# Modulation sums moved from TensorE to VectorE in a two-block transformer kernel, and gathered in the feed-forward stages and one MLP

## What is computed

```python
s_lat, s_ctx = silu(c), silu(c_ctx)[None, :]
for i in range(2):
    sh1, sc1, g1, sh2, sc2, g2 = split(s_lat @ ada_w[i] + ada_b[i], 6)       # ada_w[i]: 1024 x 6144
    csh1, csc1, cg1, csh2, csc2, cg2 = split(s_ctx @ ada_w[i] + ada_b[i], 6)
    a_l = rms_norm(h_lat, norm_g[i, 0]) * (1 + sc1) + sh1
    ...
```

## Time and profile before

| | |
|---|---|
| time, median of 3 runs | 1859.87 us (1859.79 to 1861.17) |
| the profiled execution | 1859.17 us, of which its span is 1857.4 us |
| mean granted clock of TensorE, as a share of full | 0.984 |
| busy: TensorE, weight loads, VectorE, ScalarE, GpSimd | 1758.9, 1600.3, 810.8, 890.4, 1169.6 us |
| read from memory | 295.89 MB, 160 GB/s over the span |
| groups L951 (ada, 768 records) and L959 (turn, 48 records) | 53.1 and 6.1 us busy |

### The profile page before, as it was taken

How to read it: one execution, slowest core, us unless ns; L and a number is a source line. 1 busy time by engine, 2 the same in 40 slices (tenths; PEclk the granted TensorE clock), 3 DMA queues, 4 the chain that set the end, 5 groups by cost and what they waited for, 6 DMA issues and landing times.

```text
span 1857.4 us, 32633 instructions
## 1 busy us (share of the span) xinstructions
PE 1758.9 (95%) x12970; PEld 1600.3 (86%) x12970; DVE 810.8 (44%) x1929; ACT 890.4 (48%) x1462; POOL 1169.6 (63%) x768
## 2 busy tenths in 40 slices
PE   7899999999999999999999979999999989989997
PEld 6888899999998888999999867777777777689997
DVE  6677445313366784353233662121212275642223
ACT  6535547445666345464445863131313353554443
POOL 6876678788888775778788515444434434158884
PEclk9999999999999999999999989999999999999999
DMA  6643365655556434656655514333334433135552
GB/s 235 196 134 126 125 228 199 224 207 182 182 194 195 134 115 139 241 182 216 227 182 182 166 57 148 133 136 131 137 130 148 183 114 131 40 101 191 185 183 80
DMA packets 83416, 299.06 MB, mean 161 GB/s; under 512 B 9152, under 2 KB 11456, under 8 KB 83008
## 3 DMA queue, kind: packets, MB, share of 16 engines
q1 hardware_dynamic: 81648, 294.02, 46.4%
q10 hardware_dynamic: 1616, 2.95, 0.5%
HBM read 295.89 MB, written 1.05 MB: 160 GB/s over the span
## 4 chain that ended last, share of the span: by engine, by line
PE 78%; DVE 9%; POOL 5%; ACT 3%; issue 3%; DVEq 2%; DMA 0%; ACTq 0%; SPq 0%
PE bank L937 23%; PE bank L940 22%; PE bank L941 22%; POOL wlo L886 5%; PE bank L951 2%; PE bank L1117 1%; ACT whi L1356 1%; PE bank L1133 1%; PE bank L1180 1%; DVE split_acts L1814 1%; PE bank L1103 1%; DVE acts L2026 1%; DVE acts L2067 1%; PE bank L1183 1%; PE bank L1184 1%
## 5 line engine op out<-in xcount | busy, mean ns | idle before, releaser
L886 POOL TENSOR_TENSOR wlo<-raw,whi 128x256 fp32r<-128x256 f32 (+1 forms) x756 | 1163.8, 1564 | 666.8 <-ACT whi L1356 666.5
L937 PE MATMUL bank<-split_acts,whi 128*128 128x256 f32 (+1 forms) x3492 | 1059.9, 304 | 30.0 <-DVE split_acts L1814 16.6
L940 PE MATMUL bank<-split_acts,whi 128*128 128x256 f32 (+1 forms) x3492 | 1047.4, 300 | 0.0
L941 PE MATMUL bank<-split_acts,wlo 128*128 128x256 f32 (+1 forms) x3492 | 1047.1, 300 | 0.0
L937 PEld LDWEIGHTS bank<-split_acts,whi 128*128 128x128 f32 x3492 | 670.5, 192 | 81.3 <-issue 28.9
L1356 ACT ACTIVATE whi<-raw 128x1024 fp32r<-128x1024 f32 x459 | 482.4, 1055 | 509.9 <-PE bank L937 331.1
L941 PEld LDWEIGHTS bank<-split_acts,wlo 128*128 128x128 f32 x3492 | 671.1, 192 | 20.8
L940 PEld LDWEIGHTS bank<-split_acts,whi 128*128 128x128 f32 x3492 | 671.3, 192 | 20.2
L2449 DVE SCALAR_TENSOR_TENSOR acts<-bank,acts 128x256 f32<-128x256 f32 x104 | 47.4, 482 | 227.5 <-PE bank L941 227.5
L2463 DVE TENSOR_SCALAR acts<-bank 128x512 f32<-128x512 f32 (+1 forms) x64 | 35.6, 558 | 204.7 <-PE bank L941 197.6
L1814 DVE TENSOR_TENSOR split_acts<-bank,split_acts 128x256 fp32r<-128x256 f32 (+1 forms) x212 | 97.9, 462 | 49.4 <-ACT split_acts L1500 20.7
(11 more groups left out here) (275 smaller groups left out, 1595.6 us busy)
## 6 DMA issues: line engine op xcount, KB each, us to landing
raw<-in_stream SPq DMA_DIRECT2D x555, 512.0 KB, 3.8
acts<-in_x SPq DMA_DIRECT2D x1, 1024.0 KB, 6.3
acts<-in_ctx ACTq DMA_DIRECT2D x1, 1024.0 KB, 7.4
acts<-in_const ACTq DMA_DIRECT2D x1, 1024.0 KB, 5.0
out<-acts SPq DMA_DIRECT2D x8, 128.0 KB, 2.0
acts<-in_const SPq DMA_DIRECT2D x1, 711.0 KB, 8.3
acts<-in_p ACTq DMA_DIRECT2D x2, 256.0 KB, 4.0
acts<-in_const ACTq DMA_DIRECT2D x1, 320.0 KB, 2.9
```

The lines of the kernel that those rows point to most:

```text
L886: last = nc.gpsimd.tensor_tensor(wlo[slot][:, cols], raw[source][:, cols], whi[slot][:, cols].bitcast(F32), ALU.subtract)
L937: first = nc.tensor.matmul(out_ap, w_hi, hi_act(k), start=(k == 0), stop=False)
L940: nc.tensor.matmul(out_ap, w_hi, lo_act(k), start=False, stop=False)
L941: last = nc.tensor.matmul(out_ap, w_lo, hi_act(k), start=False, stop=(k == k_tiles - 1))
```

## The change

TensorE's ada and turn tiles go. A modulation chunk ("mod") now holds two k steps of half a part, two times 128 x 512, so that four chunks (SUM_CHUNKS) make one of 24 halves. VectorE reads it from its raw slot and adds silu times weight into a running sum per side (0 context, 1 latents; halves from 16 on have side 1 alone). In block 1 the running sums are in PSUM banks 6 and 7, and the last step writes to SBUF; in block 2 they are in SBUF, in v2. The slot is freed by VectorE (mod_used). When a half is done, a "sum" tile two tiles later adds the 128 partitions on TensorE: one matmul per 128 columns and side, the sums as weights, a column of ones as moving operand. VectorE adds the bias.

The chunks are no longer in heads, middle stages and attention. Each layer of block 1 has 24 in its feed-forward stages, before hg 0,1 to 0,9, dn 0,1 to 0,6 and hg 1,0 to 1,8; block 2's first MLP has 48, before nearly every w1 and w2 tile. The bytes fetched are the same. c_square has two banks in place of four, `opening_gains` comes later in layer 1, and eight columns of constants that only the turn used are gone.

```diff
@@ -79,26 +79,23 @@
     + [("kn", j) for j in range(4)] + [("qn", j) for j in range(4)] + [("qr", 0), ("qr", 1)]
     + [("rotq", 0), ("rotq", 1)])
-ADA_TILES = DEPTH * 6 * D // 256
-LAYER_ADA = 12
-PLACES = 4
-
-
-def with_modulation(tiles, places, first, flush=()):
-
-    out, n, turned = [], first, first // PLACES
-    for t in tiles:
+SUM_CHUNKS = 4
+SUM_BEHIND = 2
+
+
+def with_sums(tiles, places):
+
+    out, n, due = [], 0, []
+    for i, t in enumerate(tiles):
+        if due and due[0][1] <= i:
+            out.append(("sum", due.pop(0)[0]))
         for _ in range(places.get(t, 0)):
-            if n // PLACES > turned:
-                out.append(("turn", turned))
-                turned += 1
-            out.append(("ada", n))
+            out.append(("mod", n))
             n += 1
-        if t in flush and n // PLACES > turned:
-            out.append(("turn", turned))
-            turned += 1
+            if n % SUM_CHUNKS == 0:
+                due.append((n // SUM_CHUNKS - 1, i + SUM_BEHIND))
         out.append(t)
-    assert turned * PLACES == n
+    assert not due
     return out, n
...
@@ -114,16 +111,14 @@
 FIRST_PRODUCT = {"mix": ("u", 0), "ffn": ("hg", 0, 0), "ple": ("pg", 0)}
 for _name in ("ffn", "ple"):
     TAIL_TILES.insert(TAIL_TILES.index(FIRST_PRODUCT[_name]) + 1, ("ss", _name))
-HEAD_TILES, _n = with_modulation(HEAD_TILES, {("u", 1): 1, ("gl", 0): 1, ("ss", "q"): 1, ("rotk", 0): 1},
-                                 0, flush=(("kn", 2),))
-MID_TILES, _n = with_modulation(MID_TILES, {("g", 2, 0): 1, ("g", 2, 2): 1, ("g", 2, 4): 1, ("g", 2, 6): 1}, _n,
-                                flush=(("y", 2, 7),))
-TAIL_TILES, _n = with_modulation(TAIL_TILES, {("hg", 0, 3): 1, ("hg", 0, 6): 1, ("hg", 0, 9): 1, ("dn", 0, 3): 1}, _n,
-                                 flush=(("dn", 0, 6),))
-assert _n == LAYER_ADA
+FFN_PLACES = {**{("hg", 0, j): 1 for j in range(1, 10)}, **{("dn", 0, n): 1 for n in range(1, 7)},
+              **{("hg", 1, j): 1 for j in range(9)}}
+ALL_TAIL_TILES, LAYER_MODS = with_sums(TAIL_TILES, FFN_PLACES)
+TAIL_TILES = [t for t in ALL_TAIL_TILES if t[0] != "mod"]
 FF_TILES = TAIL_TILES[TAIL_TILES.index(("hg", 0, 0)):TAIL_TILES.index(("dn", 1, 0))]
 PLE_TILES = TAIL_TILES[TAIL_TILES.index(("pg", 0)):]
-TILES = HEAD_TILES + MLA_FILL + FOX_FILL + MID_TILES + TAIL_TILES
+ALL_LAYER_TILES = HEAD_TILES + MLA_FILL + FOX_FILL + MID_TILES + ALL_TAIL_TILES
+TILES = [t for t in ALL_LAYER_TILES if t[0] != "mod"]
...
@@ -185,19 +176,20 @@
 def chunk_reach(tiles, spans, order, at):
-    reach, needed, adas, read = {}, 0, 0, 0
+    reach, needed, mods, read = {}, 0, 0, 0
     for t in tiles:
-        end = -(-spans.get(t, (0, 0))[1] // CHUNK_ATOMS)
+        first, to = spans.get(t, (0, 0))
+        end = -(-to // CHUNK_ATOMS)
         read = max(read, end)
-        if t[1][:2] != ("py", 0):
+        if t[1][:2] != ("py", 0) and to > first:
             needed = max(needed, end)
-        adas += ADA_CHUNKS * (t[1][0] == "ada")
+        mods += t[1][0] == "mod"
         last = at[t] if needed == read else order.index(("split", needed - 1))
         r = min(last + AHEAD, len(order) - 1)
         while r + 1 < len(order):
             kind, n = order[r + 1]
             freed_by, m = order[r + 1 - RING] if r + 1 >= RING else ("split", 0)
-            if kind == "split" and (n >= needed + SLOTS_AHEAD or (freed_by == "ada" and m >= adas)):
+            if kind == "split" and (n >= needed + SLOTS_AHEAD or (freed_by == "mod" and m >= mods)):
                 break
             r += 1
         reach[t] = r
@@ -251,15 +243,15 @@
     + [("ss", 1, 0)] + Q_TILES + K_TILES + V_TILES
     + [("o", n) for n in range(KT)]
     + [("ss", 1, 1)] + mlp_tiles(1) + [("ss", "last")])
-TILES2, _n = with_modulation(
-    TILES2,
-    {("w1", 0, 0, 0): 2, ("w1", 0, 0, 4): 1,
-     **{(w, 0, q, j): 1 for q in range(QUARTERS) for w in ("w1", "w2") for j in (0, 4) if (w, q) != ("w1", 0)},
-     ("w2", 0, 3, 2): 1, ("w2", 0, 3, 6): 1, ("w1", 0, 3, 2): 1,
-     ("q", 4): 1, ("q", 6): 1, ("k", 0): 1, ("k", 1): 1},
-    DEPTH * LAYER_ADA, flush=(("ss", 1, 0), ("k", 2)))
-assert _n == ADA_TILES
-BEFORE2 = modulation_before(TILES2)
+
+
+MLP_PLACES = [((w, 0, q, j), 1) for q in range(QUARTERS)
+              for w, js in (("w1", range(2, 7) if q == 0 else range(1, 6)),
+                            ("w2", range(8 if q < 2 else 7 if q == 2 else 5))) for j in js]
+ALL_TILES2, _n = with_sums(TILES2, dict(MLP_PLACES))
+assert DEPTH * LAYER_MODS + _n == DEPTH * 6 * KT
+BEFORE2 = modulation_before(ALL_TILES2)
+TILES2 = [t for t in ALL_TILES2 if t[0] != "mod"]
...
@@ -419,10 +410,11 @@
 def modulation_atoms(a, m):
-    group, k = divmod(m, PLACES * ADA_CHUNKS)
-    layer, part = divmod(group, 6)
-    w = a["ada_w_2"][layer][k * P:(k + 1) * P, part * D:(part + 1) * D]
-    return [w[:, i * P:(i + 1) * P] for i in range(KT)]
+    half, pair = divmod(m, SUM_CHUNKS)
+    layer, part = divmod(half // 2, 6)
+    at = part * D + half % 2 * 512
+    return [a["ada_w_2"][layer][k * P:(k + 1) * P, at + i * P:at + (i + 1) * P]
+            for k in (2 * pair, 2 * pair + 1) for i in range(4)]
...
@@ -587,6 +579,14 @@
     return ("mla", n) if n < STEPS // 2 else ("fox", n - STEPS // 2)
+LAYER_SUMS = LAYER_MODS // SUM_CHUNKS
+
+
+def sum_of(half):
+
+    return half // 2, half % 2, (0, 1) if half < 16 else (1,)
+
+
...
@@ -709,7 +708,7 @@
         low[0] = H_AT
         h = take(4096)
         pr2, pt2 = take(1024), take(1024)
-        rows2 = v2[:, 0:256]
+        mod_sums = [[v2[:, (2 * i + s) * 512:(2 * i + s + 1) * 512] for s in range(2)] for i in range(2)]
         pooled_sq = [sq2[:, i * 256:(i + 1) * 256] for i in range(KT)]
...
         k_rstd, logits2 = x, squares
-        c_square = [bank[4], bank[5], bank[6], bank[7]]
+        c_square = [bank[4], bank[5]]
+        mod_parts = [bank[6], bank[7]]
         x_squares = [bank[5], bank[6]]
...
@@ -862,7 +862,7 @@
                 if kind == "split":
                     sp.wait_ge(lo_ready, n + 1)
                 else:
-                    sp.wait_ge(ada_used, n + 1)
+                    sp.wait_ge(mod_used, n + 1)
             for c in range(N_CHUNKS - RING):
...
-            def modulation(b):
-
-                for part in range(ADA_CHUNKS):
-                    c, k = RAW_OF[("ada", Cursor.ada)], Cursor.ada % KT
-                    Cursor.ada += 1
-                    pe.wait_ge(raw_in[c % RING], (c // RING + 1) * 16)
-                    for strip in range(4):
-                        last = nc.tensor.matmul(b[32 * strip:32 * strip + 32, 0:256], silu_c[:, 2 * k:2 * k + 32],
-                                                raw[c % RING][:, strip * 256:(strip + 1) * 256],
-                                                start=(part == 0), stop=(part == ADA_CHUNKS - 1))
-                    last.then_inc(ada_used, 1)
-                return last
-
-            def turn_rows(b, rows):
-                for i in range(2):
-                    last = nc.tensor.matmul(b[:, 8 * i:8 * i + 8], rows[:, i * P:(i + 1) * P], C("strips"),
-                                            start=True, stop=True)
+            def sum_parts(b, half):
+
+                pe.wait_ge(mod_summed, half + 1)
+                for s in sum_of(half)[2]:
+                    for i in range(4):
+                        last = nc.tensor.matmul(b[:, 2 * i + s:2 * i + s + 1], tile(mod_sums[half % 2][s], i, P),
+                                                ones[:, 0:1], start=True, stop=True)
                 return last
             nc.tensor.sem_inc(slots_used, FREE_SLOTS)
             nc.tensor.sem_inc(pv_done, 1)
-            pe.wait_ge(silu_ready, 1)
             for lay in range(DEPTH):
...
@@ -1845,20 +1824,36 @@
                 v.scalar_tensor_tensor(out=p, in0=p, scalar=1.0, in1=s, op0=ALU.add, op1=ALU.mult)
                 v.drain()
-            def take_modulation(t, b, rows, group):
-                if t[0] == "ada":
-                    if t[1] % PLACES == 0:
-                        v.tensor_copy(rows, b[:, 0:256]).then_inc(tiles_out, 1)
-                    else:
-                        v.drain()
-                        v.tensor_tensor(rows, b[:, 0:256], rows, ALU.add).then_inc(tiles_out, 1)
-                    return
-
-                turned = b[:, 0:16].rearrange("p (i g s) -> p g i s", i=2, s=2)
-                m = mod[:, 16 * group:16 * group + 16].rearrange("p (g i s) -> p g i s", i=2, s=2)
-                at = PAR2["ada_b"] + KT * group
-                bias = par2[:, at:at + KT].rearrange("p (g i) -> p g i", i=2).unsqueeze(3).broadcast_to([P, 4, 2, 2])
-                v.tensor_tensor(m, turned, bias, ALU.add).then_inc(tiles_out, 1)
+            def modulation_sum(n):
+
+                half, pair = divmod(n, SUM_CHUNKS)
+                c = RAW_OF[("mod", n)]
+                dve.wait_ge(raw_in[c % RING], (c // RING + 1) * 16)
+                sides = sum_of(half)[2]
```

(36 more changed lines are left out.)

75 lines of the change are left out of this document (31 added, 44 removed).

## The result

The changed kernel takes 2052.58 us, the median of 4 runs (2047.37 to 2055.71), beside 1859.88 for the kernel before: ratio 1.1032, 95% interval 1.1012 to 1.1051. The forecast was 1995, its range ended at 2050: the sign and the main loop held, the size fell short. The profiled execution is the fastest of the four, 2047.37 us with a span of 2045.5; the other three lie at 2052 to 2056, so a few microseconds of the median are in no trace here.

A forecast was written before the change was run, and what follows sets the result against it. The prediction took TensorE, busy 95%, to bound the kernel before, and a loop of waits to slow the changed one. On 1859.17 us: -67 + 19 + 171 + 4 + 4 + 6 = +137, 1996, given as 1995; range 1915 to 2050.

The forecast's parts named there:

- the main loop: Feed-forward halves: VectorE's late slot release delays fetches, ScalarE's split, tanh and the next modulation chunk; 171 us in both layers.
- L: Feed-forward halves: length of the loop from one modulation chunk's end to the next; 10.1 to 13.2 us, 11.2 taken.
- the third transfer: Feed-forward loop: last of three fetches a modulation chunk held up; lands at 6.8 us, split before hu's high copy.
- M: A modulation chunk in the feed-forward order; VectorE's 3.0 us of sums on it free its raw slot late.
- term of 171 for the halves: Feed-forward halves, both layers: 171 us added by a loop of 11.2 us (132 at 10.1, 243 at 13.2).
- The heads and the middles: Heads: 8 ada tiles hidden, earlier second-head transfers save 6 us in all; exposed ada tiles elsewhere save 1.40 each.
- The M in dn 0, n = 1 to 6: Down product 0: TensorE's 3.96 us against VectorE's 0.4 + 3.0, no ScalarE result; costs 0 to 8 us, 4 taken.
- the cold clock: Feed-forward stages: TensorE starts cold after gaps, a few us at each of four ends, 4 in all.
- the forecast's formula: Feed-forward halves: half 0 takes 5.7 + 9L against 61.6 us, half 1 7.3 + 9L against 67.4.
- costed at nothing: Feed-forward stages: 12 sum tiles, 192 records, 29 us if exposed, taken as free because TensorE idles there.
- Block 2's first MLP: Block 2: no loop closes; sum tiles cost 19 us, stalls beside GpSimd 0 to 30, 6 taken.
- L stays: Part of the slower rival (15%): same loop length, feed-forward and down products at 1.2 GHz; +64, 2059 at most.

The follow-up runs named there:

- lag2: The changed kernel, but in block 1 ScalarE need not split into a slot held by a modulation chunk of the last two tiles; 1880.33 us, ratio 1.0114.
- ctxfirst: The changed kernel with ScalarE squaring the context ahead of the splits for the same tile in layer 1's dn 0; 2024.98 us.
- before2banks: The kernel before the change with two banks for the context squares in place of four; 1860.39 us.
- late: The changed kernel with block 1's sum tiles four tiles behind their half's last chunk instead of two; 2034.46 us (one run).

## Why the prediction was short

- **What bounds it, the mechanism: right.** The slot that VectorE frees late, SP in order, ScalarE in order, the tanh and the high copy behind a split: every link stands in the chain above. L was taken as 11.2 and is 11.2. The forecast's way through the third transfer had it landed 6.8 us after the slot is free and the next M ended at 11.8; in the chain these are 6.1 and 11.2. (The longest L, given as 13.2, comes to 13.1 from its own terms; nothing hangs on that.) lag2, which cuts only the link from ScalarE to the slot, gives back 172 us. That this equals the forecast's term of 171 for the halves is chance: in the traces lag2 takes 141 us out of the four halves and 25 out of layer 1's dn 0, where the forecast had no loop.
- **The heads and the middles: right.** Forecast -6 for the two heads and -12.2 for the middles' 8 ada and 2 turn tiles, -18; measured -16.4.
- **The step that failed: "The M in dn 0, n = 1 to 6, find 3.96 us of TensorE against 0.4 + 3.0 of VectorE, and no ScalarE result".** It gave the down products 0 to 8 us, 4 taken, and ScalarE "two tiles of room". Less the 3.8 of the ada and turn tiles that go there this is about 0; measured +1.8 in layer 0 and +36.6 in layer 1. The context squares are a ScalarE result, in layer 1 alone, and they close the loop a second time; ctxfirst takes 28.4 of it away, and its chain shows the circle in what is left. I had counted the squares' banks (rightly nothing, by before2banks) and not their place behind the splits.
- **The halves: slightly short.** 171 for the loop and 4 for the cold clock, less 8.4 for 6 ada tiles: 167. Measured 41.0 + 45.8 + 39.7 + 50.2 = 176.7. By the forecast's formula each half should add about 40.7 (half 0 with its 3 ada tiles taken off). The halves 0 do, 41.0 and 39.7; the halves 1 add 45.8 and 50.2. late shows a second term that was mis-sized: the sums were costed at nothing "because by the next part TensorE idles there", but behind the last M of half 1 it does not, and moving them takes 11.8 us out of the two halves 1.
- **Block 2's first MLP: too careful.** 20 ada and 5 turn tiles go (30.5), 19 for the sums and 6 for stalls come: -5.5. Measured -12.6. A record there takes 0.11, not 0.15: 5 us. The stalls beside GpSimd are there, but TensorE is busy 351.4 of 353 us beside them: 6 us. These two come to 11 where the difference is 7, so some 4 us were lost elsewhere in the sum; no run here says where.
- **Attention: too hopeful.** 4 ada tiles and a turn taken out, -6.1 with nothing against it; it rises by 0.7. TensorE waits there for others, 18.7 us in gaps over 0.4 in the changed kernel and 13.6 before, so that what I had costed as exposed was hidden; this is read from the two traces and not tested.

Together, against the forecast of +137: dn 0 38, the halves 10, MLP -7, attention and the second MLP 7, heads and middles 2 come to 50 more, the +187 seen. The range was too narrow by 2.6 us of the median, since a second loop had no place in it: the bounds of the down products were worked out from TensorE's and VectorE's times. One rival, "L stays" with the down products at 1.2 GHz, reached 2059 and so has the measured time under it, but by luck: layer 0's dn 0 takes 38.2 us, and layer 1's takes 44.7 once the square is moved. TensorE's share was given as about 55%; it is 61% in the window above, at a mean clock of 0.78, since part of its matmuls run at the lower level, 1.2 GHz.

## What to carry to other kernels

When work is moved to an engine whose end frees a buffer, walk from that buffer round every in-order queue back to the engine; the time is the circle's length, and the busy shares don't show it (in the window of half 0 no engine was busy over 61%). List each result that an engine gives behind its prefetching work, in every layer and not only in the layer one reads; each closes a circle of its own. The cure was no faster engine but a prefetch that keeps off slots still in use (172 of 193 us), and the best version moves only the second layer's modulation, into a stage where no circle closed (0.9938 of the kernel before).

## What the hardware showed beside this

The later transfers of a burst land late: the third of three 5.3 to 5.9 us after its issue in the first chain above, the second 4.6 and 4.1 in layer 1's dn 0, the median of all being 3.7. And the sums in SBUF: the two forms of the chunk's operations, min/median/max in ns, in PSUM and in SBUF:

```profile
L1840 DVE TENSOR_SCALAR bank<-raw,acts x24: 743/750/756, 310.5 to 1136.5; 128x512 f32<-128x512 f32 x24
L1840 DVE TENSOR_SCALAR acts<-raw,acts x16: 472/486/2569, 1320.8 to 1631.4; 128x512 f32<-128x512 f32 x16
```

```profile
L1842 DVE SCALAR_TENSOR_TENSOR bank<-raw,acts,bank x144: 747/752/758, 312.0 to 1172.1; 128x512 f32<-128x512 f32 x144
L1842 DVE SCALAR_TENSOR_TENSOR acts<-raw,acts x112: 740/752/2889, 1321.8 to 1651.2; 128x512 f32<-128x512 f32 x112
```

With the sum in PSUM no operation is ever longer than 0.76 us. In SBUF both forms stand up to 2.1 us longer than their median, about one GpSimd low part (2.4 us), and the plain multiply is otherwise faster, 0.49 us. The timelines tie the two together: 25 of these 128 operations take over 0.9 us, and every one of them ends 0.55 us (sum) or 0.28 to 0.29 us (plain multiply) after the end of a GpSimd low part. Of the 168 operations on the PSUM sums 89 lie wholly inside a GpSimd instruction, and none is longer for it. I had not expected the one-input form to stand. The Trainium skill, "SBUF — State Buffer", Who interferes with whom, says that tensor_scalar can enter a mode that takes the port pair shared with GpSimd for the whole instruction, and its rule that a single SBUF input does not contend leaves that mode out, a condition that the prediction did not give. The 0.49 beside the 0.75, and the 2.57, agree.
